# A mixture-of-experts stage whose weight pieces are issued from one engine's queue or from two

## The reference

```python
def expert_choice_ffn(h, w_router, w_gate, w_up, w_down):
    xf = h.reshape(-1, shp[-1]); n = xf.shape[0]
    cap = CAPACITY_FACTOR * n // N_EXPERTS          # 64 latent or 16 context tokens per expert
    aff = jax.nn.softmax((xf @ w_router).astype(jnp.float32), axis=-1)
    gate, idx = lax.top_k(aff.T, cap)
    xs = xf[idx]
    hid = silu(einsum('ecd,edf->ecf', xs, w_gate)) * einsum('ecd,edf->ecf', xs, w_up)
    ye = einsum('ecf,efd->ecd', hid, w_down) * gate[..., None]
    y = jnp.zeros_like(xf).at[idx.reshape(-1)].add(ye.reshape(-1, shp[-1]))
```

## Time and profile before

| | before |
|---|---|
| median of 3 runs | 2833.48 us (2830.31 to 2840.59) |
| profiled execution | 2829.18 us |
| its span, first to last instruction | 2827.2 us |
| mean granted TensorE clock | 0.985 |
| TensorE busy | 2701.8 us (96%) |
| ScalarE busy | 865.2 us (31%) |
| VectorE busy | 1418.9 us (50%) |
| expert pieces issued by SyncE | 384, 1024 KB each |
| HBM read / written | 649.88 MB / 31.65 MB |

### The profile page before, as it was taken

One profiled execution on the slowest core, in us unless ns is written; L12 is line 12 of the kernel. 1 busy time (PEld: TensorE's weight loads), 2 busy tenths in 40 slices (PEclk: granted clock), 3 DMA queues, 4 the chain that ended last, 5 costly groups with the idle time before them and its releaser, 6 DMA issues.

```text
span 2827.2 us, 45585 instructions
## 1 busy us (share of the span) xinstructions
PE 2701.8 (96%) x18423; PEld 1664.3 (59%) x18423; DVE 1418.9 (50%) x2366; ACT 865.2 (31%) x1618; POOL 143.7 (5%) x206
## 2 busy tenths in 40 slices
PE   7999899999899999999999996999999999999995
PEld 5878668898678888888888883333332222232221
DVE  4446777788878878888775554111111111111103
ACT  4336444444754344434434432001000000000002
POOL 0000000000000000000013001000000000000000
PEclk9999999999999999999999998999999999999998
DMA  9832113443024444444465329999999999999997
GB/s 350 304 120 75 55 58 119 140 136 108 1 90 156 147 166 164 152 162 149 167 234 195 119 108 349 400 401 399 388 397 399 399 399 401 401 391 401 399 412 268
DMA packets 175136, 684.01 MB, mean 242 GB/s; under 512 B 14548, under 2 KB 14756, under 8 KB 119164
## 3 DMA queue, kind: packets, MB, share of 16 engines
q1 hardware_dynamic: 159504, 613.45, 57.0%
q0 software_dynamic: 13392, 67.79, 7.8%
q10 hardware_dynamic: 2064, 0.26, 0.1%
HBM read 649.88 MB, written 31.65 MB: 241 GB/s over the span
## 4 chain that ended last, share of the span: by engine, by line
PE 76%; DMA 11%; SPq 8%; DVE 4%; issue 1%; ACT 1%; POOL 0%; POOLq 0%; DVEq 0%; ACTq 0%
PE ps L1039 41%; PE ps L1542 9%; DMA ar<-w_exp_up 8%; SPq L686 5%; PE ps L1058 5%; PE ps L1551 4%; PE ps L1588 4%; PE ps L1065 3%; SPq L688 2%; PE ps L1596 2%; DMA hT<-w_exp_down 1%; DMA ar<-w_exp_down 1%; DMA ring<-w_mod 1%; PE ps L985 1%; PE ps L1320 1%
## 5 line engine op out<-in xcount | busy, mean ns | idle before, releaser
L1039 PE MATMUL ps<-split_weights,split_tokens 128*128 128x512 f32 x5040 | 1160.0, 391 | 4.9 <-DVE split_tokens L563 4.6
L1039 PEld LDWEIGHTS ps<-split_weights,split_tokens 128*128 128x128 f32 x5040 | 943.2, 188 | 212.0 <-issue 10.1
L556 ACT ACTIVATE split_weights<-ring 128x512 fp32r<-128x512 f32 x368 | 232.7, 632 | 672.7 <-PE ps L1039 596.9
L560 DVE TENSOR_TENSOR split_weights<-ring,split_weights 128x512 fp32r<-128x512 f32 x368 | 255.5, 694 | 324.0 <-ACT split_tokens L557 320.4
L1993 ACT ACTIVATE ar<-ps 128x512 f32<-128x512 f32 x16 | 9.6, 599 | 915.9 <-PE ps L1542 915.9
L1542 PE MATMUL ps<-ar 128*32 128x512 f32 x2304 | 263.4, 592 | 4.1 <-DMA ar<-w_exp_up 4.1
L563 DVE TENSOR_TENSOR split_tokens<-hT,split_tokens 128x640 fp32r<-128x640 f32 x288 | 237.3, 824 | 0.0
L2502 DVE TENSOR_TENSOR ar<-ps,ar 16x512 f32<-16x512 f32 x64 | 44.0, 688 | 350.0 <-PE ps L1596 349.3
L429 DVE SCALAR_TENSOR_TENSOR cst<-ring,cond,cst 128x512 f32<-128x512 f32 x300 | 213.1, 746 | 0.0
L557 ACT ACTIVATE split_tokens<-hT 128x640 fp32r<-128x640 f32 x288 | 208.4, 724 | 0.0
L2487 DVE SCALAR_TENSOR_TENSOR ar<-ar,gateT,ps 48x512 f32<-48x512 f32 x16 | 12.1, 754 | 377.8 <-ACT ar L1995 377.8
(11 more groups left out here) (363 smaller groups left out, 2415.0 us busy)
## 6 DMA issues: line engine op xcount, KB each, us to landing
ring<-w_mod SPq DMA_DIRECT2D x96, 1024.0 KB, 5.7
ar<-w_exp_up SPq DMA_DIRECT2D x80, 1024.0 KB
ar<-w_exp_down SPq DMA_DIRECT2D x72, 1024.0 KB
ar<-w_exp_gate SPq DMA_DIRECT2D x64, 1024.0 KB
ring<-w_in SPq DMA_DIRECT2D x60, 1024.0 KB, 5.2
hT<-w_exp_gate SPq DMA_DIRECT2D x48, 1024.0 KB
hT<-w_exp_down SPq DMA_DIRECT2D x40, 1024.0 KB
hT<-w_exp_up SPq DMA_DIRECT2D x32, 1024.0 KB
```

The source lines that it names most:

```text
L556: self.eng.activation(spW[:, s, 0, :], raw, ACT.Copy)
L560: a = self.eng.tensor_tensor(spW[:, s, 1, :], raw, spW[:, s, 0, :].bitcast(F32), ALU.subtract)
L1039: mm = pe.matmul(ps[:, b, :], spX[:, s, x, b * P:(b + 1) * P], spW[:, s, w, :], start=(k == 0 and x == w), stop=(k == n_k - 1 and x == 1))
```

## The change

Of the stream's pieces from 16 on, those with an even number are issued by SyncE as before, those with an odd number by ScalarE. Slots, sizes, semaphores and the counts that are waited for stay. The issuing function becomes `expert_load(eng, n, g)`, which both engines call.

On ScalarE seven issues stand ahead of the silu of an expert (pieces 17, 19, ... 29 counted from the expert's first; the last of them waits until pair 6 of this expert is used) and five behind the copies (pieces 31 to 39; the last waits until the expert is done). ScalarE's loop now runs over pairs of experts, with two bodies written out.

```diff
+        def expert_load(eng, n, g):
+            if type(n) is not int or 2 * EXP_G * n + g >= ESLOTS:
+                eng.wait_ge(exp_used, n * (2 * EXP_G) + (g + 1 - ESLOTS))
+            eng.sem_inc(loads_issued, 1)
+            at, j, s = ds(n * 2 + g // EXP_G, 1), g % EXP_G, g % ESLOTS
+            if j < 16:
+                src = (w_eg, w_eu)[j % 2][at, j // 2, :, :, :].squeeze(0)
+                eng.dma_start(exp_slot[s].rearrange("p (k n) -> p k n", k=2), src).then_inc(exp_ready[s // 2], 16)
+            else:
+                eng.dma_start(exp_slot[s], w_ed[at, :, down_order[j - 16], :].squeeze(0)).then_inc(exp_ready[s // 2], 16)
...
             with sync.Fori(0, NE // 2 - 1) as n:
-                for g in range(ESLOTS, 2 * EXP_G + ESLOTS):
+                for g in range(ESLOTS, 2 * EXP_G + ESLOTS, 2):
                     expert(n, g)
-            for g in range(ESLOTS, 2 * EXP_G):
+            for g in range(ESLOTS, 2 * EXP_G, 2):
                 expert(NE // 2 - 1, g)
...
-            def expert_act(e, last):
+            def expert_act(n, b, last):
+                e, g = n * 2 + b, EXP_G * b
+                for at in range(g + ESLOTS + 1, min(g + ESLOTS + 14, 2 * EXP_G) if last else g + ESLOTS + 14, 2):
+                    expert_load(act, n, at)
                 silu(e)
...
                 copy_xs(xs_parts[2])
-
-            with act.Fori(0, NE - 1) as e:
-                expert_act(e, False)
-            expert_act(NE - 1, True)
+                for at in range(g + ESLOTS + 15, g + ESLOTS + 24, 2):
+                    expert_load(act, n, at)
+
+            with act.Fori(0, NE // 2 - 1) as n:
+                for b in range(2):
+                    expert_act(n, b, False)
+            expert_act(NE // 2 - 1, 0, False)
+            expert_act(NE // 2 - 1, 1, True)
```

More of the change, by code:

```diff
@@ L633, in k4 @@
                 return v.rearrange("p (k n) -> p k n", k=4)
-            def k2(v):
-                return v.rearrange("p (k n) -> p k n", k=2)
             for t in range(NT):
@@ L678, in expert @@
             def expert(n, g):
[L680 to L688, removed]
+                expert_load(sync, n, g)
             sync.wait_ge(slot_used, SLOTS + G_OUT + 16)
```

## The result

| | before | after |
|---|---|---|
| median | 2835.69 us (20 runs) | 2841.94 us (20 runs, 2838.51 to 2847.13) |
| ratio, 95% interval | | 1.0027 [1.0020, 1.0034] |
| profiled execution's span | 2827.2 us | 2839.9 us |

Two of the 20 runs before took 4635 and 9746 us, for which the record has no reason, and the ratio leaves them out; the other 18 lie between 2828.49 and 2841.26 us.

What follows compares the result with a forecast made beforehand. The prediction took the total work of the DMA engines as the bound. Its terms, +3 for the gather and +1 for order of landing, summed to +4 us; on a median of 2833.48 us it forecast 2837 us, range 2820 to 2852.

Steps and rivals of the forecast that it cites:

- A: Whole kernel: the DMA engines stay the bound and nothing much moves; 2837 us, own range 2826 to 2848, chance 0.72.
- The plain stream, 0: Weight loads with nothing else beside them: 421 GB/s with one queue or two, so 0 us.
- The gather, +3: Gathers of token rows beside two weight queues: +0.2 us each, over 15 gathers +3 us, bounds -25 and +17.
- the total stays: Bound for one gather: total rate stays at 243 GB/s, the gather lasts 8.2 us and costs 1.1 us more.
- the weights take up the rest: Bound for one gather: its packets keep their time, the total rises to 365 GB/s, and it costs 1.7 us less.
- The adding back, 0: Adding back of results on GpSimd's queue: lands some 4 us later, cost to the stream unchanged, 0 us.
- ScalarE ahead of silu and behind the copies, 0: ScalarE's issues before silu just hidden, or covered by TensorE's spare time; later issues covered by pieces in flight: 0 us.
- Rival B: ScalarE is held at an issue ahead of silu, as SyncE is at some issues: slower, 2859 us, chance 0.07.
- Order of landing, +1: Odd pieces run ahead of even ones, so the last pairs land differently: +1 us, bounds 0 and +13.
- the last expert, 0: Residual's loads get a third of the stream, but bytes ahead of the last piece stay: 0 us, bounds -5 and 0.
- Rival C: Gathers cost the stream more beside two weight queues (+17 us), or even pieces fall behind (+13): 2851 us, chance 0.09.
- D: The gather's loss shrinks (-25 us), or a second queue keeps the engines better fed: faster, 2812 us, chance 0.09.

Runs made afterwards that it cites:

- split_tail: The changed kernel with only the last 32 pieces split between SyncE and ScalarE, all earlier ones by SyncE: 2834.47 us, 1.0001 against the kernel before.
- split_quarter: The changed kernel with ScalarE issuing only every fourth piece and SyncE the other three: 2842.09 us, 1.0024 against the kernel before.
- sync_all: The changed kernel, ScalarE's loop over pairs of experts kept, with all pieces issued by SyncE again: 2833.66 us, 0.9996 against the kernel before.
- split_head: The changed kernel with the last 32 pieces all issued by SyncE, the split kept everywhere else: 2842.65 us, 1.0033 against the kernel before.

## Why the prediction was right, and what in it was not

The time was inside the range and the sign was that of the forecast: +4 us forecast, +6 to +8 measured. That the sum came so near is in part luck: its +3 for the gather was less than half of what the gather came to cost, and of its +1 for the order of landing nothing was found. Step by step:

- *The DMA engines are the bound and stay it* (A): right. Shares of 1.02 in both stages, waits of 33.7 us for "near 32" from 2175 us on (and 3.2 us more ahead of it), 421 GB/s between gathers.
- *The plain stream, 0*: right, and the one thing that no row showed directly. The rule of the Trainium skill, "DMA: Bandwidth & Descriptors", section "Rules for kernel authors", that spreading DMAs over engines doesn't help bandwidth holds here: 421 GB/s with one hardware queue and with two.
- *The gather, +3*: the term that was mis-sized. That it would last 8.2 us was right (8.28), and of the two bounds, "the total stays" (+1.1) and "the weights take up the rest" (-1.7), the first was near: the total rose from 282 to 290 GB/s only. It was +0.61 us a gather by packets, 14 gathers, +8.5 us; by bytes 7.4 us. I took +0.2 as a middle of two mechanisms, though the row said which one holds: the weights' packets themselves were slow. The 243 GB/s of the earlier trace rows was also that of 4 us within one gather; over whole gathers the mean is 282.
- *The adding back, 0*: right in cost (3.07 us before and after). It lands later, by 1.5 us in the median; 4 were forecast:

```profile
ar<-x_scaled_rows,gidx POOLq DMA_INDIRECT x16, 12.9
y_rows<-ar,sidx POOLq DMA_INDIRECT x15, 12.2
```

These are the medians from issue to landing after; before they were 10.4 and 10.7 us.
- *ScalarE ahead of silu and behind the copies, 0*: right. Silu came 2.22 us behind pair 6, a little over the "1.9 to 2.1", TensorE waited no longer for it, and no issue of ScalarE was held, so the reserve of the second stage wasn't needed. Rival B fell: with two queues neither is full.
- *Order of landing, +1, and the last expert, 0*: `split_tail` put both at -0.2 us, inside its interval of -2.3 to +2.6. Whether it grows when one queue has more to bring (`split_quarter`) is open.
- *Rival C*, the gather dearer, was the mechanism, at half of its price; D had its sign wrong. The prediction looked for the cause in how the total rate is shared; that the slow rate goes with gathers into fewer than 128 partitions (3.55 us for 80 rows, 2.49 for 128), no step of it had.

## What to carry over

Here a second queue added nothing to a stream that already filled the DMA engines, and long issues of the engine that feeds it were no cost. What changed is the share that every other transfer gets: the one that slows the packets beside it lasted longer and so cost more. Look for the transfer beside which the neighbours' packets are slow. Here it was a gather into 80 of 128 partitions, and fetching 48 rows for nothing bought 15 us, twice what the change had cost.

## What the runs showed that was not expected

Weight packets are slowed by another queue's gather (470 ns for 314 ns), but not by another queue's accumulating writes (318 ns), whose own packets take 628 ns.

The 3.8 us ahead of the change go with TensorE's clock. Both kernels do the same work there; in columns of the earlier trace rows, first before, then after:

```profile
325.00:340.00 15.00, 13.18 (x102) 8.01 (x101) 13.46 (x27) 4.85 (x11) 1.08 (x2) 0.95 0.05 19
```

```profile
325.00:340.00 15.00, 13.93 (x84) 8.67 (x85) 10.67 (x21) 3.51 (x8) 1.08 (x2) 0.59 0.05 19
```

The mean granted clock was 0.95 and 0.59, so that most of the second stretch ran at the lower level, 1.2 GHz: 16 products of 64 rows took 3.68 us there for 1.95 us. Products that start 0.03 us apart in the two profiles at 321.6 us are 3.6 us apart at 340 us, so nearly all of the 3.8 us arise there. Ahead of it TensorE had waited again and again for single steps of VectorE, in both kernels. `split_tail` had the low clock there too (0.62), and its first expert piece comes at 1688.73 us; `sync_all` and `split_head` didn't (0.91), with 1683.35 and 1686.44 us. So it isn't an effect of the change. The span of a single profiled execution carries such a difference; the distance from a common point, as the first expert piece, does not.
